# A decoder layer on one core: the first modulation in two portions, the first projections chunk by chunk, the last gate inside the feed-forward

## What is computed

```python
mod = silu(c) @ w_ada + b_ada                    # 6 x 1024: sh1, sc1, g1, sh2, sc2, g2
h = rms_norm(x, g_pre_mix) * (1 + sc1) + sh1
proj = h @ w_in                                  # 1024 x 6536, split into q, k, v of three branches,
                                                 # index queries and keys, and 3 x 1024 gate logits
o_sb, o_mb, o_ds = three causal attentions       # 6, 5 and 5 heads of 64; the last keeps 64 keys per query
g = sigmoid(gate_logits + b_gate)
merged = g_sb * (o_sb @ w_sb) + g_mb * (o_mb @ w_moba) + g_ds * (o_ds @ w_dsa)
x = x + g1 * rms_norm(merged @ w_o, g_post_mix)
h = rms_norm(x, g_pre_ffn) * (1 + sc2) + sh2
gate, up = split(h @ w_up)                       # 1024 x 5632
x = x + g2 * rms_norm((silu(gate) * up) @ w_down, g_post_ffn)
```

## Time and profile before

| | us |
|---|---|
| median of 3 runs | 470.22 (469.19 to 470.88) |
| the profiled execution | 469.08 |
| its span, first to last instruction | 467.3 |
| busy in the span: TensorE | 439.0 (94%) |
| VectorE / ScalarE / POOL | 317.6 (68%) / 237.6 (51%) / 27.5 (6%) |

### The profile page before, as it was taken

The page is one execution under the profiler, slowest core; times in us unless marked ns, Lnnn a source line. Parts: engine busy times, 40 slices in busy tenths (PEclk is TensorE's granted clock), DMA queues, the critical chain, the costliest instruction groups (busy, mean ns, idle before and its releaser), DMA issues.

```text
span 467.3 us, 7634 instructions
## 1 busy us (share of the span) xinstructions
PE 439.0 (94%) x2927; PEld 388.4 (83%) x2927; DVE 317.6 (68%) x550; ACT 237.6 (51%) x419; POOL 27.5 (6%) x60
## 2 busy tenths in 40 slices
PE   0949999999999999999989999999999999999994
PEld 0529999999889989998988898888888888888883
DVE  2057679768399969685898458885775595586535
ACT  6046646547576655676555339554253344435231
POOL 2001002100023140000000000000000000000000
PEclk9979999999999999999999999999999999999998
DMA  8997898596956774856478801996556637520002
GB/s 297 426 369 241 284 305 291 182 319 225 333 167 210 256 271 171 286 195 200 142 242 302 311 2 43 366 371 209 186 173 187 242 116 249 194 90 1 1 0 90
DMA packets 56818, 99.86 MB, mean 214 GB/s; under 512 B 5212, under 2 KB 41684, under 8 KB 53716
## 3 DMA queue, kind: packets, MB, share of 16 engines
q1 hardware_dynamic: 54132, 81.62, 51.1%
q0 software_dynamic: 2656, 17.84, 11.0%
HBM read 98.39 MB, written 1.06 MB: 213 GB/s over the span
## 4 chain that ended last, share of the span: by engine, by line
PE 88%; DMA 4%; DVE 3%; ACT 2%; SPq 1%; issue 1%; DVEq 0%; ACTq 0%; PEldq 0%
PE psum L1322 18%; PE psum L1323 17%; PE psum L1324 17%; PE psum L1618 16%; PE psum L1619 8%; DMA ada_end<-in_w_ada_dram 4%; PE psum L1582 3%; PE psum L1473 1%; DVE wlo L956 1%; PE psum L1412 1%; PE psum L1410 1%; PE psum L1444 1%; PE psum L1455 1%; PE psum L1379 1%; ACT whi L653 1%
## 5 line engine op out<-in xcount | busy, mean ns | idle before, releaser
L1618 PE MATMUL psum<-hcut,whi 128*128 128x512 f32 x320 | 111.7, 394 | 0.0
L1322 PE MATMUL psum<-hcut,whi 128*128 128x256 f32 (+1 forms) x360 | 105.9, 294 | 3.4 <-DVE hcut L1069 2.7
L1323 PE MATMUL psum<-hcut,whi 128*128 128x256 f32 (+1 forms) x360 | 102.4, 285 | 0.0
L1324 PE MATMUL psum<-hcut,wlo 128*128 128x256 f32 (+1 forms) x360 | 102.4, 284 | 0.0
L956 DVE TENSOR_TENSOR wlo<-raw,whi 128x1024 fp32r<-128x1024 f32 (+4 forms) x84 | 76.5, 936 | 21.2 <-ACT whi L653 20.9
L1619 PE MATMUL psum<-hcut,wlo 128*128 128x256 f32 x320 | 88.8, 277 | 0.0
L653 ACT ACTIVATE whi<-raw 128x1024 fp32r<-128x1024 f32 (+4 forms) x84 | 66.2, 822 | 20.9 <-DMA raw<-in_w_in_dram 16.4
L1322 PEld LDWEIGHTS psum<-hcut,whi 128*128 128x128 f32 (+1 forms) x360 | 68.9, 191 | 8.4 <-issue 3.2
L1618 PEld LDWEIGHTS psum<-hcut,whi 128*128 128x128 f32 x320 | 60.0, 188 | 13.9
L1323 PEld LDWEIGHTS psum<-hcut,whi 128*128 128x128 f32 (+1 forms) x360 | 69.0, 192 | 0.0
L1324 PEld LDWEIGHTS psum<-hcut,wlo 128*128 128x128 f32 (+1 forms) x360 | 68.9, 191 | 0.0
(11 more groups left out here) (186 smaller groups left out, 672.3 us busy)
## 6 DMA issues: line engine op xcount, KB each, us to landing
raw<-in_w_up_dram SPq DMA_DIRECT2D x22, 1024.0 KB, 7.6
xn<-in_w_ada_dram POOLq DMA_DIRECT2D x16, 1024.0 KB, 5.1
raw<-in_w_in_dram SPq DMA_DIRECT2D x7, 2048.0 KB, 9.2
draw<-in_w_down_dram SPq DMA_DIRECT2D x11, 1024.0 KB, 5.0
raw<-in_w_in_dram SPq DMA_DIRECT2D x4, 1280.0 KB, 6.7
raw<-in_w_in_dram SPq DMA_DIRECT2D x3, 1536.0 KB, 7.8
raw<-in_w_ada_dram SPq DMA_DIRECT2D x2, 2048.0 KB, 9.7
ada_end<-in_w_ada_dram SPq DMA_DIRECT2D x4, 1024.0 KB, 16.9
```

Of the source, the lines that this page charges most:

```text
L1322: pe.matmul(dst, a[0], b[0], start=first, stop=False)
L1323: pe.matmul(dst, a[0], b[1], start=False, stop=False)
L1324: return pe.matmul(dst, a[1], b[0], start=False, stop=last)
L1618: pe.matmul(dst[:, :], wh, hcut[:, k, :, :].rearrange("p a s -> p (a s)"), start=k == 0, stop=False)
```

## The change

*First modulation.* `w_ada`'s first third is loaded in two portions: columns 0 to 511 of shift and of scale, then columns 512 to 1023. The second portion goes into the same buffer, pair of chunks by pair, when its products are done. Blocks 0 to 3 of `w_in` become eight chunks of the depth, each 128 rows by 1224 columns for all of units 0 to 9, loaded in three DMAs. The order on SP is: first portion, chunks 0 to 3, second portion, chunks 4 to 7, then the blocks as before. The six vectors are loaded from ScalarE's queue.

`x` is turned unscaled and kept; the inverse root of each token is turned into a row instead, and one operation multiplies a chunk by scale column and root row, another adds the shift. A modulated chunk is cut at once. TensorE multiplies chunk by chunk, all ten units for one chunk, into five banks; the second portion's products stand inside chunks 2 and 3:

```diff
+            for k in range(KC):
+                if k % 4 == 0:
+                    load_ada(k // 4)
+                load_chunk(k)
...
+            for k in range(KC):
+                act.wait_ge(chunk_in[k], 48)
+                act.activation(chunk_view(whi, end_hi, k), chunk_view(raw, None, k), ACT.Copy).then_inc(w_hi, 2)
+                if k == 4:
+                    keep_row(1)
+                act.wait_ge(tmp_ready, k + 1)
+                act.activation(hhi[:, k, :], htmp[k % 2], ACT.Identity, bias=col[0][:, k:k + 1]).then_inc(chunk_hi, 1)
...
+            def chunk_columns(c0, c1):
+                n, sums = c1 - c0, mod_columns(int(c0 in (0, 4)))[:, :, c0 % 4:c0 % 4 + c1 - c0]
+                scale, base = col[0][:, KC + c0:KC + c1], VEC_ADA + KC + c0
+                then(dve.tensor_tensor(scale, sums[:, 1, :], vecs[:, base:base + n], ALU.add))
+                then(dve.tensor_tensor(scale, scale, vecs[:, VEC_PRE_MIX + c0:VEC_PRE_MIX + c1], ALU.mult))
+                then(dve.tensor_tensor(col[0][:, c0:c1], sums[:, 0, :], vecs[:, VEC_ADA + c0:VEC_ADA + c1], ALU.add))
...
+            for k in range(KC):
+                if k == 0:
+                    dve.wait_ge(mod_first, 1)
+                    chunk_columns(0, 1)
+                elif k == KC // 2:
+                    chunk_cut_lo(k)
+                    dve.wait_ge(mod_turned, 2)
+                    chunk_columns(4, 8)
+                chunk_scaled(k)
+                if k != KC // 2:
+                    chunk_cut_lo(k)
+                chunk_rest(k)
+                if k == 0:
+                    dve.wait_ge(mod_turned, 1)
+                    chunk_columns(1, 4)
...
+            PRODUCTS_AT = {(2, 9): (0, 1), (3, 5): (2, 3)}
+            for p in range(KC // 2):
+                row_products(0, p)
+                if p < KC // 2 - 1:
+                    warm_up(8)
...
+            for k in range(1, KC):
+                pe.wait_ge(w_hi, 2 * (k + 1))
+                pe.wait_ge(w_lo, 2 * (k + 1))
+                pe.wait_ge(chunk_hi, k + 1)
+                pe.wait_ge(chunk_lo, k + 1)
+                for u in range(FIRST_UNIT):
+                    mm = first_unit(u, k)
...
+                    for p in PRODUCTS_AT.get((k, u), ()):
+                        row_products(1, p)
+                    if (k, u) == (3, 9):
+                        turn_row(1)
```

*Projections.* A memset for the second block waits for the units only; three of its four low cuts stand before the first gated tile, the fourth behind it; later pieces stand directly behind their gated tile:

```diff
-            for q in range(4):
+            p, chunks, cols = block_parts(B_PROJ + 1)[3]
+            dve.wait_ge(units, N_UNITS)
+            dve.memset(block_view(wlo[(B_PROJ + 1) % 2], B_PROJ + 1)[HD:P, chunks, cols].bitcast(F32), 0.0)
+            for q in range(3):
                 cut_lo(B_PROJ + 1, q)
             for f in range(KC - 1):
-                pieces = MERGE_PIECES[f] if f else []
+                pieces = MERGE_PIECES[f] if f else [(1, 3)]
                 gate_tile(f)
-                for b, q in pieces[0:1]:
+                for b, q in pieces:
                     cut_lo(B_PROJ + b, q)
...
-                for b, q in pieces[1:]:
-                    cut_lo(B_PROJ + b, q)
```

*Last gate.* `g2` is summed in the feed-forward. POOL loads a part of 1024 columns at a time, VectorE adds it behind steps 1 to 8, ScalarE and VectorE cut the sum, and TensorE sums over the partitions with ones, which also spreads it to all rows:

```diff
+            def gate_part_sum(i):
+                dve.wait_ge(gate_bias_in, 16)
+                dve.wait_ge(gate_done, i)
+                dve.wait_ge(gate_in, 16 * i)
+                dve.scalar_tensor_tensor(gsum, gpart, csil_all[:, bass.ds(i - 1, 1)], gsum, ALU.mult, ALU.add).then_inc(gate_done, 1)
...
             with dve.Fori(1, N_FFN - 2, 2) as i:
                 step(i, 0, False)
+                gate_part_sum(i)
                 step(i + 1, 1, False)
+                gate_part_sum(i + 1)
...
+                for n in range(2):
+                    cols = slice(BANK * n, BANK * (n + 1))
+                    pe.matmul(bank[B_UP[0][n]][:, :], ones[:, :], whi[1][:, cols], start=True, stop=False)
+                    mm = pe.matmul(bank[B_UP[0][n]][:, :], ones[:, :], wlo[1][:, cols], start=False, stop=True)
...
+            for n in range(2):
+                cols = slice(BANK * n, BANK * (n + 1))
+                then(dve.tensor_tensor(gb[2][:, cols], gb[2][:, cols], bank[B_UP[0][n]][:, :], ALU.mult))
             for t in range(TT):
                 add_residual(1, t)
```

More of the change, by code:

```diff
@@ L88, in mix_units @@
     features(2, T_QMB, W_MB - HD)
-    keys(3, T_QMB, T_KMB, W_MB)
+    features(3, T_KMB, W_MB - HD)
+    units.append((3, "last head", W_MB - HD, P, (T_QMB + W_MB // P, T_KMB + W_MB // P)))
     tokens(4, "values", 0, W_MB, V_MB)
@@ L181, in pieces_at @@
     plan = {}
-    for b in range(N_MIX):
+    for b in range(FIRST_BLOCK, N_MIX):
         us = [n for n, u in enumerate(UNITS) if u[0] == b]
@@ L241, in raw_arrivals @@
 def raw_arrivals():
[L243 to L246, removed]
+    count, out = [0, 0], {}
+    for b in range(FIRST_BLOCK, B_FFN):
+        count[b % 2] += 16 * LOADS[b]
+        out[b] = count[b % 2]
     return out, count
 RAW_ARRIVED, RAW_COUNT = raw_arrivals()
-RAW_OF_BLOCK = {b: r for r, (kind, b) in enumerate(RAW) if kind == "block"}
 def decoder_layer(nc, x, c, w_ada, b_ada, g_pre_mix, g_post_mix, w_in, b_gate, w_proj_sb,
@@ L908, in step @@
             def step(i, slot, first, last):
-                if not last:
-                    for q in range(4 if first else 2):
-                        cut_up_hi(i + 1, 1 - slot, q, first)
+                if not last and not first:
+                    for q in range(2):
+                        cut_up_hi(i + 1, slot, q)
                 silu_tile(i, slot, 0, first)
@@ new lines, in turn_row @@
+            def turn_row(half):
+                pe.wait_ge(row_kept, half + 1)
+                if half == 0:
+                    pe.wait_ge(pick_ready, 1)
+                    pe.wait_ge(x_kept_act, 1)
+                    pe.wait_ge(x_kept_dve, 1)
+                for c in range(4):
+                    dst = bank[7 if half or c == 0 else 6]
+                    mm = pe.matmul(dst[:, 2 * c:2 * c + 2], mrow[:, P * c:P * (c + 1)], pick[:, :], start=True, stop=True)
+                    if half == 0 and c == 0:
+                        mm.then_inc(mod_first, 1)
+                mm.then_inc(mod_turned, 1)
@@ new lines, in first_unit @@
+            def first_unit(u, k, passes=(0, 1, 2)):
+                b, what, c0, n, dest = UNITS[u]
+                base = CHUNK_COLS - P if what == "last head" else CHUNK_BASE[b] + c0
+                wh, wl = [chunk_view(x, ends, k)[:, base:base + n] for x, ends in ((whi, end_hi), (wlo, end_lo))]
+                products = ((wh, hhi), (wh, hlo), (wl, hhi))
+                for i in passes:
+                    w, h = products[i]
+                    mm = pe.matmul(first_place(u)[0:n, :], w, h[:, k, :], start=k == 0 and i == 0 and u in (1, 2, 4, 6, 8),
+                                   stop=k == KC - 1 and i == 2, skip_group_check=True)
+                return mm
@@ L1487, in _ @@
+            for u in range(FIRST_UNIT, N_UNITS):
                 unit(u)
-                if u == 2:
-                    pe.wait_ge(unit_read, 1)
+                if u == FIRST_UNIT:
                     pe.wait_ge(col_ready, 1)
```

683 lines of the change are left out of this document (405 added, 278 removed).

## The result

| | before | after |
|---|---|---|
| median of 4 runs each | 470.06 us | **465.75 us** (465.28 to 466.61) |
| ratio after : before, 95% interval | | 0.9917, 0.9897 to 0.9936 |
| the profiled execution, its span | 469.08, 467.33 | 465.32, 463.58 |

The change makes the kernel 4.3 us faster, where 8.6 were forecast from the median shown. 465.75 lies inside the range of 456.5 to 466 and outside the forecast's own, 459 to 464.5. The profiled executions differ by 3.76 us against a sum of 7.95.

A forecast was written before the change was run, and what follows sets the result against it. TensorE's chain bounds the kernel, so only an earlier start or fewer gaps help: 6.0 + 0.4 + 0.1 + 1.7 + 0.7 - 0.95 = 7.95 off 469.08 gives 461.1, plus 0.5: 461.6 us; 8-in-10 range 456.5 to 466.

The forecast's parts named there:

- Steps of unchanged length: Feed-forward steps: the last gate's eight sums fit VectorE's 5.21 us idle per step, so they cost nothing.
- The start: Up to the end of unit 9: done at 58.2 instead of 64.2 us, gain 6.0, bounds 2.7 to 8.8.
- half clock for the first stretch, and none for the 3.35 us behind the wait: TensorE's start: 1.2 GHz in the first stretch from 21 us costs 1.8 us; nothing lost behind the wait before chunk 4.
- Order at the second portion: Start, before chunk 4: row kept, turned, made columns and scaled in a chain; chunk 4 multiplied from 44.1 us.
- Units: Units after the start: the 0.47 us stall at 181 us goes, gain 0.4, bounds -4 and +0.5.
- rival (b): Units 10 to 18: TensorE waits 4 us for cuts of block 5 or 6, 465.6 us; chance 0.15.
- Projections: Projections: VectorE's gated product comes 1.7 us earlier, gain 1.7, bounds 0.7 to 2.7; one turning less adds 0.1.
- First step: First feed-forward step: TensorE starts chunk by chunk without the 0.70 us gap, gain 0.7, bounds -0.5 and 0.8.
- Last gate: Near TensorE's end: four added matmuls of 512 columns, -0.95 us on the path; the eight sums cost nothing.
- (a): Start: clock holds from the first product, DMA keeps 426 GB/s, unit 9 ends at 55.4, 458.8 us; chance 0.15.
- (c): Start: short rows keep DMA under 290 GB/s, unit 9 ends after 66.2, gains elsewhere gone; chance 0.05.
- (d): Feed-forward: the last gate's sums hold it, 9.6 us back, no change, 471 us; chance 0.03.

The follow-up runs named there:

- `clock_kept`: The changed kernel with 20 idle products of 128 columns in TensorE's wait before chunk 4: 463.96 us, 0.9875 of the kernel before.
- the five edits: Changed kernel with row products spread over chunk 3, row kept and turned sooner, VectorE's columns before its cut, chunk 4 multiplied pass by pass: 462.89 us.

## Why the prediction was wrong, step by step

- **Steps of unchanged length: wrong, -1.9 us, the largest part.** The prediction named it as a sign of failure, but only the sums had been weighed as a cause, and they are innocent. The chain of causes is shown from its first link to its last but one: small tiles ahead in memory, down buffers 64 bytes on, a longer rhythm of the up products. Nothing in the rows of before shows it but the second step, whose pairs take 0.353 us there too. The Trainium skill (TensorE: Matmul & The Clock Gate, Wait — 56ns, not 53.3ns?) gives a matmul 2.5 ns over its columns at 2.4 GHz, measured there with bf16 back to back; an estimate by it is 325 ns for the pair. The rows disagree, for matmuls with a weight load each: 347 or 353 ns, by the place.
- **The start: 4.35 of 6.0.** First product 21.73 (21 forecast), chunk 4 landed 38.7 (37), chunk 4 multiplied 44.20 (44.1). The step that failed is "half clock for the first stretch, and none for the 3.35 us behind the wait". It came the other way round: 1.00 from 21 to 41 us, 0.53 from 44 to 47, and 1.5 of the missing 1.65 us are that. The time of chunk 4 came out right by luck: the waits around chunks 0 and 1, the later first product and a chain of 3.7 us in place of 3.35 made up what the first stretch did not lose. The prediction priced the fall behind the wait (1.8 us more; 1.5 came) and did not choose it. For the first stretch it overlooked that the change itself puts idle products (`warm_up`) into the waits for `w_ada`; no run leaves them out, so that they held the clock is not shown. The Trainium skill's rule (the same page, What's actually happening: throttled by default, released by activity) agrees with `clock_kept`, where idle products alone held the clock, and with both starts, where the first turnings stand 0.21 us apart and later ones 0.11. The prediction held the full clock "from 9 to 25 us" against that rule; it took the window's 1.00 at its word, and the turnings from 11.68 to 15.5 us ran at half. By the time of the first dense products, 21.73 us, TensorE had the full clock already.
- **Order at the second portion.** The forecast followed the chain (ScalarE keeps the row behind chunk 4's high part, VectorE cuts before it makes columns) and took it as given; with the five edits chunk 4 comes 2.1 us sooner (44.20 to 42.11).
- **Units: -0.5 in place of +0.4.** The stall at 181 us went; one of 0.28 us came at 128.67, where VectorE's cuts stand behind a sum of 1.28. The tight units 10 to 13 held, so rival (b) fell. Some 0.4 of it are the yardstick: each logit pair also slows the matmuls at its two ends (0.09 and 0.10 us), and 64.2 counted two pairs without that; the start's gain is then as much smaller.
- **Projections: 1.34 of 1.8**, within the bounds. No gap of 1 us is left; the largest are of 0.35 and 0.54 us (235.90 and 249.79), and the profile names no releaser for either.
- **First step: +0.95, forecast 0.7**, gap gone as said. **Last gate: right**, four matmuls of 0.23 us at 448 us. **Tail**: 0.5 us less up to the end of the last store; not forecast, not studied.
- **Rivals.** Of (a) a part came: the clock held from the first product to the wait before chunk 4, but DMA did not keep 426 GB/s. (c) and (d) fell: 350 GB/s from 21 to 41 us, and no sum holds a step.

## What to carry to other kernels

When a change adds or removes a tile, however small, compare the distance of equal matmuls in the main loop before and after: if it differs with the engine busy throughout and the clock the same, move the buffers before looking for an engine to blame. A wait of TensorE can cost more than its length: one of 2.66 us here cost 1.5 us of half clock behind it, those of about 0.6 us at the start none. If it can't be closed, try idle products in it. And check a window's granted clock at the start of a trace against the distance of equal matmuls. Where a chain of small steps crosses three engines, look first at what each of them does ahead of its own step.

## What the runs showed of the hardware

The distance of up products of 512 and 256 columns depends on where buffers stand that *other* products of the loop read: 0.347 or 0.353 us with the same instructions on the same addresses, stable from step to step in the kernels before and after. The down products themselves depend on it too, 5.47 to 5.60 us for 24. Together, steps take 16.57 to 16.91 us for shifts in units of 32 bytes. A start on a multiple of 256 bytes is no remedy (16.78 with 96 bytes of padding). Idle products of 128 columns hold the granted clock at 1.00 through a wait at the end of which it otherwise falls to one half.
